# A hybrid encoder step with a 32-expert MoE: the last three experts finished in slots, and casts and products on GpSimd

## What is computed

```
def hier_moe(x, ...):                      # x = rms_norm(h), T = 1056 rows
    group = argmax(group logits)           # 4 groups of 8 experts
    two best experts of that one group, with gates that sum to g_top
    for each expert e, rows of its tokens:
        y = (silu(x @ w_gate[e]) * (x @ w_up[e])) @ w_down[e]
        out[token] += gate * y
h = h + hier_moe(rms_norm(h))
y = rms_norm(h) * norm_final_g             # mean of squares of a row, eps, root
```

## Time and profile before

| | us |
|---|---|
| median of the runs | 1858.48 |
| lowest and highest of 3 | 1855.87 and 1858.67 |
| span of the profiled execution | 1853.7 |
| TensorE busy | 1785.6 (96%) |
| last matmul starts | 1825.8 |
| last store of a tile issued | 1839.2 |

### The profile page before, as it was taken

One profiled execution on the slowest core, in us unless ns is written; L12 is line 12 of the kernel. 1 busy time (PEld: TensorE's weight loads), 2 busy tenths in 40 slices (PEclk: granted clock), 3 DMA queues, 4 the chain that ended last, 5 costly groups with the idle time before them and its releaser, 6 DMA issues. The chain is left out here.

```text
span 1853.7 us, 25673 instructions
## 1 busy us (share of the span) xinstructions
PE 1785.6 (96%) x10105; PEld 1550.8 (84%) x10105; DVE 1063.0 (57%) x1244; ACT 780.6 (42%) x918; POOL 510.4 (28%) x284
## 2 busy tenths in 40 slices
PE   8999999999999999999999979989999999999993
PEld 6989989999999999999999978857777777767772
DVE  7565580001455445554621142367888888889886
ACT  5455460000122111221300023227778878777875
POOL 0422322222222222222233310012233433323331
PEclk9999999999999999999999989999999999999997
DMA  4111111223111111111122366558999999999986
GB/s 149 38 52 52 32 55 61 73 73 117 49 38 34 37 37 44 41 34 37 39 87 95 120 208 225 210 203 307 366 380 369 379 369 371 378 368 379 366 318 236
DMA packets 146290, 316.24 MB, mean 171 GB/s; under 512 B 10986, under 2 KB 106314, under 8 KB 121496
## 3 DMA queue, kind: packets, MB, share of 16 engines
q1 hardware_dynamic: 135896, 287.74, 42.6%
q0 software_dynamic: 10304, 27.24, 5.3%
HBM read 287.72 MB, written 36.08 MB: 175 GB/s over the span
## 5 line engine op out<-in xcount | busy, mean ns | idle before, releaser
L222 PE MATMUL job_ps<-xn_hi,w_hi 128*128 128x352 f32 x1488 | 494.9, 333 | 0.3 <-issue 0.3
L224 PE MATMUL job_ps<-xn_hi,w_lo 128*128 128x352 f32 x1488 | 478.7, 322 | 0.0
L223 PE MATMUL job_ps<-xn_lo,w_hi 128*128 128x352 f32 x1488 | 478.0, 321 | 0.0
L206 POOL CAST w_hi<-w_raw 128x1024 fp32r<-128x1024 f32 x78 | 85.6, 1097 | 774.4 <-issue 467.3
L222 PEld LDWEIGHTS job_ps<-xn_hi,w_hi 128*128 128x128 f32 x1488 | 280.0, 188 | 4.1 <-issue 1.0
L223 PEld LDWEIGHTS job_ps<-xn_lo,w_hi 128*128 128x128 f32 x1488 | 280.6, 189 | 2.5 <-issue 0.3
L224 PEld LDWEIGHTS job_ps<-xn_hi,w_lo 128*128 128x128 f32 x1488 | 279.9, 188 | 0.0
L2289 DVE TENSOR_TENSOR ex_raw_lo<-ex_raw,ex_w_hi 128x2048 fp32r<-128x2048 f32 x88 | 200.0, 2285 | 13.4 <-ACT ex_w_hi L2192 13.3
L208 POOL TENSOR_TENSOR w_lo<-w_raw,w_hi 128x1024 fp32r<-128x1024 f32 x78 | 205.0, 2629 | 6.3
L2192 ACT ACTIVATE ex_w_hi<-ex_raw 128x2048 fp32r<-128x2048 f32 x88 | 168.8, 1918 | 57.1 <-PE ex_y L2066 24.5
L754 DVE TENSOR_TENSOR gate<-job_ps,gate 128x352 f32<-128x352 f32 x48 | 25.2, 525 | 288.6 <-PE job_ps L224 288.6
(11 more groups left out here) (327 smaller groups left out, 3379.9 us busy)
## 6 DMA issues: line engine op xcount, KB each, us to landing
ex_raw<-in_w_chunks SPq DMA_DIRECT2D x88, 1024.0 KB, 20.3
u<-in_w_chunks SPq DMA_DIRECT2D x52, 1024.0 KB, 17.8
raw_more<-in_w_chunks SPq DMA_DIRECT2D x52, 1024.0 KB, 19.3
w_raw<-in_w_in SPq DMA_DIRECT2D x64, 512.0 KB, 4.0
merged_lru<-gate SPq DMA_DIRECT2D x8, 528.0 KB, 5.2
spare<-merged_lru SPq DMA_DIRECT2D x8, 528.0 KB, 5.9
merged<-gate SPq DMA_DIRECT2D x8, 528.0 KB, 5.0
w_raw<-in_w_lru_o SPq DMA_DIRECT2D x8, 512.0 KB, 4.4
```

What stands on the lines that cost most here:

```text
L206: pool.tensor_copy(M.w_hi[s][:], M.w_raw[s][:]).then_inc(M.hi_done[s], 1)
L222: pe.matmul(out, M.w_hi[s][:, k, :], x_hi[:, k, cols], start=(k == 0), stop=False)
L223: pe.matmul(out, M.w_hi[s][:, k, :], x_lo[:, k, cols], start=False, stop=False)
L224: mm = pe.matmul(out, M.w_lo[s][:, k, :], x_hi[:, k, cols], start=False, stop=(k == KD - 1))
```

## The change

- The last three experts are finished in slots, not the last two: ADDED is expert 29. h in DRAM is complete when the add of expert 28 has landed. Chunks.ID puts input experts 31, 7 and 15 at the last three places (three groups). Expert 29's weighted rows are added to its h rows by one operation of VectorE.
- SP issues each load of a tile of h when its buffer is free, from the landing of that add on. So the loads come one expert earlier, and ScalarE's squares stand among its work on experts 30 and 31 (last_step). Roots and reciprocals are made for several tiles at once.
- GpSimd casts the chunks (31,3), (30,5) and (31,5) (POOL_CASTS), and multiplies the tiles at places 0, 1, 2 and 4 with g_fin (BY_POOL); for those VectorE only multiplies with the reciprocal.
- The transposes of expert 31's hidden rows stand between the two halves of down of expert 30, and their split goes to the buffers of x.
- The work of weigh_over is spread over experts 16 to 22, that of sample_rows goes from 22 to 24.
- GpSimd's indirect writes are six instead of four at the end.

```diff
-    ID = [e for e in range(E) if e != PER_GROUP - 1] + [PER_GROUP - 1]
+    ID = [e for e in range(E) if e not in (PER_GROUP - 1, 2 * PER_GROUP - 1)] + [PER_GROUP - 1, 2 * PER_GROUP - 1]
+    IN_SLOTS = (E - 3, E - 2, E - 1)
...
-        ADDED = E - 2
+        ADDED = IN_SLOTS[0]
+        POOL_CASTS = ((LAST, 3), (LAST - 1, 5), (LAST, 5))
...
+        BY_POOL = (0, 1, 2, 4)
+        BATCHES = ((0, 3), (3, 6), (6, NTILE + 1), (NTILE + 1, NTILE + 2), (NTILE + 2, NTILE + 3))
...
     def sync(sp):
         sp.wait_ge(y_added, 16 * ADDED)
-        for t in LAST_FIRST:
-            sp.dma_start(fin[t][0:n_rows(t), :], h_rows[span(t), :]).then_inc(h_in[t], 16)
+        for i, t in enumerate(LAST_FIRST):
+            sp.wait_ge(used, N_CHUNKS - RAW + 1 + (i if i < 4 else i + 2) // 2)
+            sp.dma_start(fin[i][0:n_rows(t), :], h_rows[span(t), :]).then_inc(h_in[i], 16)
...
     def gpsimd(pool):
         pool.wait_ge(y_added, 16 * ADDED)
-        for e in (ADDED, LAST):
+        for k, e in enumerate(IN_SLOTS):
             pool.wait_ge(x_turned, 2 * e + 2)
-            indirect(xe[e % XE][0:SLOTS, :], None, h_rows, row[e % ROWS], T - 1).then_inc(rows_in, 16)
+            indirect(base[k][0:SLOTS, :], None, h_rows, row[e % ROWS], T - 1).then_inc(rows_in[k], 16)
+        def cast(e, c):
+            n = AT[e, c]
+            pool.wait_ge(H.raw_in[n % RAW], 16 * (n // RAW) + 16)
+            pool.wait_ge(used, n - SPLIT + 1)
+            pool.tensor_copy(w_hi[n % SPLIT][:], raw[n % RAW]).then_inc(pool_hi_done, 1)
+        for ec in POOL_CASTS:
+            cast(*ec)
+        pool.wait_ge(g_in, 16)
+        for i in BY_POOL:
+            x = fin[i][0:n_rows(LAST_FIRST[i]), :]
+            pool.wait_ge(sq_done, i + 1)
+            pool.tensor_tensor(x, x, g_fin[0:n_rows(LAST_FIRST[i]), :], ALU.mult).then_inc(gained, 1)
...
         pool.wait_ge(sample_stored, 16)
+        for k in range(N_SLOTS - 1):
+            put_sample(k)
         pool.wait_ge(out_stored, 16 * NT)
+        for k in range(N_SLOTS - 1):
+            put_prompt(k)
+        put_sample(N_SLOTS - 1)
+        put_prompt(N_SLOTS - 1)
...
     def tensor(pe):
             elif s == LAST:
+                down(s - 1, lambda: turn_h(LAST))      # between its two halves
...
     def scalar(act):
+        def last_step():
+            act.wait_ge(ss_set, 1)
+            act.wait_ge(used, N_CHUNKS - RAW + 6)
+            square_tile(0)
+            hi(LAST - 1, 4)
+            silu(LAST)
+            h_part(LAST - 1)
+            square_tile(1)
+            square_tile(2)
+            act.activation(warm[:], R.eps[0:1, :], ACT.Sqrt)
+            hi(LAST, 4)
+            root(0)
+            h_part(LAST)
+            for i in range(3, 6):
+                square_tile(i)
...
     def vector(dve):
+        def scaled_tile(i):
+            n = n_rows(LAST_FIRST[i])
+            x = fin[i][0:n, :]
+            if i not in BY_POOL:
+                scaled(x, x, n, i, out_done)
+                return
+            dve.wait_ge(rstd_done, batch_of(i) + 1)
+            dve.wait_ge(gained, BY_POOL.index(i) + 1)
+            dve.tensor_scalar(x, x, rstd[0:n, i:i + 1], None, ALU.mult).then_inc(out_done, 1)
...
+        lo(LAST, 4)
+        turned_round(0)
+        h_part(LAST)
+        lo(LAST, 5)
         dve.wait_ge(g_in, 16)
+        dve.wait_ge(used, AT[LAST - 1, 5] + 1)
+        for m in range(N2):
+            add_rows(1, m, py[m])
+        turned_round(1)
+        for i in range(6):
+            scaled_tile(i)
+        turned_round(2)
+        for m, src in enumerate((pg, pu)):
+            dve.wait_ge(used, AT[LAST, 4 + m] + 1)
+            add_rows(2, m, src)
+        for i in range(6, NTILE):
+            scaled_tile(i)
```

More of the change, by code:

```diff
@@ L2094, in turn_h, with down @@
             ins.then_inc(h_turned, 1)
-        def down(e):
+        def down(e, between=lambda: None):
             pe.wait_ge(h_lo_done, e + 1)
@@ L2099, in down @@
             for i, c in enumerate((4, 5)):
+                if i:
+                    between()
                 n = AT[e, c]
@@ L2123, in down_last @@
                         kk = 2 * i + k
-                        ins = three(out[0:SLOTS, :], h_hi[:, kk, :], h_lo[:, kk, :], hi[:, k, at], lo[:, k, at],
+                        ins = three(out[0:SLOTS, :], x[:, kk, :], x_low[:, kk, :], hi[:, k, at], lo[:, k, at],
                                     kk == 0, kk == KF - 1)
@@ L2230, in scalar @@
                 out(s - 2)
+            if s == LAST:
+                last_step()
+                break
             hi(s, 3)
@@ L2237, in scalar @@
                 hi(s - 1, 5)
[L2238 to L2260 removed]
+            hi(s + 1, 0)
+            x_part(s + 1)
+            hi(s + 1, 1)
+            hi(s + 1, 2)
         def behind():
@@ new lines, in scaled_rows @@
+        def scaled_rows(k):
+            scaled(done[k], base[k][0:SLOTS, :], SLOTS, NTILE + k, rows_done)
+        dve.wait_ge(y_done, N2 * (ADDED + 1))
+        dve.wait_ge(rows_in[0], 16)
+        dve.tensor_tensor(base[0][0:SLOTS, :], base[0][0:SLOTS, :], y[ADDED % 2][0:SLOTS, :],
+                          ALU.add).then_inc(rows_added, 1)
+        lo(LAST, 4)
+        turned_round(0)
+        h_part(LAST)
+        lo(LAST, 5)
+        dve.wait_ge(g_in, 16)
+        dve.wait_ge(used, AT[LAST - 1, 5] + 1)
@@ L2373, in behind @@
+        for m in range(N2):
[7 more added lines that the diff above has]
+            add_rows(2, m, src)
+        for i in range(6, NTILE):
+            scaled_tile(i)
+        scaled_rows(0)
+        turned_round(3)
+        scaled_rows(1)
+        turned_round(4)
+        scaled_rows(2)
         def behind():
@@ L2374, in behind @@
             for i, t in enumerate(LAST_FIRST):
-                x = al[t][0:n_rows(t), :]
+                n = n_rows(t)
+                x = al[t][0:n, :]
                 dve.wait_ge(al_rms, i + 1)
-                scaled(x, x, n_rows(t), t, al_rstd, i, al_done)
+                dve.reciprocal(rstd[0:n, t:t + 1], rms[0:n, t:t + 1]).then_inc(al_rstd, 1)
+                dve.wait_ge(al_rstd, i + 1)
+                dve.scalar_tensor_tensor(out=x, in0=x, scalar=rstd[0:n, t:t + 1], in1=g_fin[0:n, :],
+                                         op0=ALU.mult, op1=ALU.mult).then_inc(al_done, 1)
```

205 lines of the change are left out of this document (114 added, 91 removed).

## The result

The changed kernel takes 1877.41 us, the median of four runs (1874.44 to 1878.88), beside 1858.27 us for the kernel before (four runs, 1855.87 to 1858.67). The ratio is 1.0105 with a 95% interval from 1.0091 to 1.0119: some 19 us slower. The profiled execution of the changed kernel took 1877.87 us and spans 1875.9 us.

What follows compares the result with a forecast made beforehand. From 1300 us, DMA engines 0.9 and more busy and TensorE hardly idle were taken as near their limit. First tile at 1818 plus 54 gave 1872, 18.3 us behind 1853.7; added to the median, 1877 us, range 1857 to 1882 (0.85).

Steps and rivals of the forecast that it cites:

- The held ScalarE: In last_step, ScalarE's square of tile 0 waits for its load before cast (30,4); TensorE starts down(30) after 12 us idle.
- The landing itself: First tile of h lands at 1818, behind weights and g_fin in SP's queue; bounds 1801 and 1823.
- the 1.2 us for the gathers: Before the weights are in, GpSimd's queue gives each of 16 DMA engines (48 - 29) / 16 = 1.2 us more.
- the term of g_fin: Norm weights g_fin, queued behind the last chunk, add 1.3 us before the first tile's own 0.3 us.
- From the span to the time: The recorded span of 1853.7 us was 4.8 us under the median 1858.48; the change was added to the median.
- Overflow lists: TensorE's 3.2 us wait at 1631 goes but returns as waits for weights: taken as 0, bounds -3.2 and 0.
- The hold-off: GpSimd's casts and products beside VectorE's two-input instructions add to them; end at 1872, against 1867 without it.
- The casts: Each chunk cast moved to GpSimd takes 2 x 1.04 = 2.1 us and adds to VectorE's two-input instructions.
- what is late next is lo(31,5): Transposes between the halves of down(30) do not win the 1.8 us before the last product; lo(31,5) is late next.
- (a): Rival: the first tile lands early and ScalarE isn't held, hold-off stays; end 1861.6, time 1866; chance 0.14.
- (b): Rival: ScalarE is held, but GpSimd's work hides beside VectorE; end 1867, time 1872; chance 0.14.
- (c): Rival: neither held ScalarE nor hold-off; end 1852.5, time 1857, no change; chance 0.11.

Runs made afterwards that it cites:

- late squares: The changed kernel with ScalarE's squares of the first tiles behind its expert work and VectorE's first reciprocals behind its last subtraction: 1868.75 us.
- lists spread only: The kernel before with only the overflow lists' work spread over experts 16 to 22 and sample_rows at 24: 1856.99 us, ratio 1.0000.
- slots only: The changed kernel with the first tiles' squares behind the weights, all casts on ScalarE and all products on VectorE: 1863.15 us, ratio 1.0036.
- two more edits: The slots only kernel with GpSimd's gathers issued after the last weight chunk landed, and VectorE scaling three tiles before the second batch of roots: 1858.61 us.

## Why the prediction was right, step by step

**The held ScalarE** was right in place and nature, and taking it away gives 7.8 to 8.7 us. That is less than the 12.3 us wait, because TensorE then stands for late weights in the same place: 4.3 us in the kernel with late squares. The sum for it counted from the tile's landing, and the chain behind it ran as worked out. From the landing, us: split of h(30) done at 4.0 by the sum, 3.9 in the trace; cast (31,4) done 9.8, 9.5; TensorE restarts 6.9, 6.8, after 12 us, 12.3; second half of down(30) done 15.4, 14.7; last subtraction done 19.9, 19.1; TensorE ends 24, 23.6; last tile scaled 37.8, 35.7; last put 46.0, 44.5; end 54, 53.3.

**The landing itself** was the mis-sized term: 1818 by the sum, 1822.6 in the trace, near the bound of 1823. The term that was too small is the 1.2 us for the gathers: their 48 engine-us (busy time summed over the DMA engines), less the 29 of the add that went, spread over all 16. The total was right: in 1796 to 1822 GpSimd's queue took 10.8% of the 16, 45 engine-us. So was the term of g_fin: it landed at 1822.0, 1.3 us behind the last chunk at 1820.7, and the tile 0.6 behind that (0.3 by the sum). But the last chunk came 5.5 us later than before, and the experiments give 4.7 and 5.4 us to the gathers (4.5 and 4.1 against the kernel with the lists spread only). That is the bound in which all of it falls on the eight engines that hold the backlog (48 / 8 = 6.0); the trace does not show which engine carries what, so this is the size that fits, and not a mechanism shown. Turns taken between the two queues would be another reason: three tiles on GpSimd's queue also made the last chunk 3.6 us later. That the tile stands in the queue's order was right: 27.1 us in SyncE's queue, 6.9 in GpSimd's. The Trainium skill, "DMA: Bandwidth & Descriptors", section "Queues, rings and completion order", says that an engine takes one queue's descriptors in ring order and takes turns between queues; both numbers agree with it.

**From the span to the time** there was an error the other way. I added the 4.8 us by which the profiled span stood under the median. But in the runs here a time lies 1.7 to 2.3 us over its own span, so that span can only be that of the run of 1855.87 us, 2.2 over it; in the changed kernel it is 2.0. The span came 3.9 us over the forecast of 1872, the offset 2.8 under: that 1877 was met within half a us is luck: two errors nearly cancel.

**Overflow lists**: taken as 0, measured 1.0000. Right, with the waits handed on as described.

**The hold-off** was right: the last subtraction 4.5 us instead of 2.3, a product between. Its price, 5 us by the sum (1872 against 1867), is 5.3 by the spans and 4.6 by the medians, but 2.8 by the ratios. **The casts** on GpSimd take 1.90 us, not 2.08, and when the square no longer holds ScalarE they are hidden but for about 1.4 us, which is within the noise. The last one, beside VectorE's subtraction, takes 2.67.

**The transposes**: "what is late next is lo(31,5)" held; alone they win nothing.

**The rivals.** (a), the tile early with the hold-off left, 1866, is the kernel with the first tiles on GpSimd's queue: 1867.7. That looks closer than it is, for (a) put the span at 1861.6 and it is 1866.9: (a) let the weights come on time, and there the chunk (30,4) took 38.0 us and TensorE waited 3.70 for it. (b), ScalarE held and products hidden, 1872, is not what happens, but products taken away come near it, 1872.8, with a span of 1870.6 instead of 1867. (c), neither, 1857, was too low: slots only takes 1863, and (c) left out the weights' delay. Its VectorE part also left out that the tiles wait for the second batch of roots. What would have met 1857 needs two more edits (1858.6).

**The half gain of late squares** was a miss of my first theory after the result: it subtracted the wait and held everything behind it fixed. The last subtraction, taken as 4.5 us, was held for 11.4 in that profile, by a row of four products. That is 6.9 of the 12 us by which its span missed 1859.

## What to carry to other kernels

- A first instruction that waits for data of the next stage, set ahead of work that a busier engine waits for, can hold that engine for nearly the whole wait (12.3 of 16.3 us here); look at the queue in which its load stands, not at the load's size.
- Work given to an idle engine is only hidden if the two engines do not hold each other off: where they do, price it as added to the other engine's instructions.
- Where transfers are near their limit, a few row gathers put among the last weights cost more than their mean share; size them by the engines that are behind.

## What the runs showed that was not expected

- The same pair of instructions was held for different lengths. VectorE's subtraction stood through one product of GpSimd in two kernels (4.52 and 4.48 us) and through four in another (11.43 us), though in each its row begins 0.06 us behind the first product's. What decides it stays open: there is one profile of each.
- Three gathers of 96 rows delayed chunks of 1 MB by 4.7 to 5.4 us, while the nine loads of h issued at the same time behind the chunks in their own queue delayed them by 0.8 at most (40.7 against 39.9, and none at (30,4)).
- A load of 32 rows took 27.1 us in SyncE's queue and 6.9 us in GpSimd's, issued within 0.4 us of the same time.
- A short wait can bring the half clock. In the changed kernel TensorE stood 1.79 us before 1812.55, and its granted clock was 0.50 from 1813.4 to 1816.4; in the kernel before it stood 1.76 us before 1820.41, and the clock stayed at 1.00. What decides it stays open. The two stretches, changed kernel first:

```profile
1813.40:1816.40 3.00, 3.00 (x9) 1.95 (x8) 0.00 (x0) 0.00 (x0) 0.64 (x1) 0.50 0.75 303
```

```profile
1822.00:1824.00 2.00, 2.00 (x11) 1.37 (x10) 1.93 (x5) 1.73 (x4) 0.00 (x0) 1.00 1.04 315
```
